# Row-64 key products, two weight cuts on GpSimd, and a looser order of cuts and PSUM banks in a four-layer fp32 block stack

## The reference

```
q = concat([q_nope, q_rope]); k = concat([k_nope, broadcast(k_rope)])     # 128 + 64 features
s = einsum('bhqd,bhkd->bhqk', q, k) / sqrt(192)
```

## Time and profile before

| what | us |
|---|---|
| median of three runs (3249.62 to 3250.29) | 3249.62 |
| the profiled execution | 3250.29 |
| its span | 3249.0 |
| PE busy | 3220.7 |
| DVE busy | 1823.7 |
| ACT busy | 1233.5 |
| POOL busy | 371.0 |

### The profile page before, as it was taken

One profiled execution on the slowest core, in us unless ns is written; L12 is line 12 of the kernel. 1 busy time (PEld: TensorE's weight loads), 2 busy tenths in 40 slices (PEclk: granted clock), 3 DMA queues, 4 the chain that ended last, 5 costly groups with the idle time before them and its releaser, 6 DMA issues.

```text
span 3249.0 us, 36841 instructions
## 1 busy us (share of the span) xinstructions
PE 3220.7 (99%) x15016; PEld 2673.2 (82%) x15016; DVE 1823.7 (56%) x2387; ACT 1233.5 (38%) x1838; POOL 371.0 (11%) x288
## 2 busy tenths in 40 slices
PE   8999999999999999999999999999999999999999
PEld 7788888888878888888888888888888888888887
DVE  3775556665477645666656643447545654345754
ACT  3222343344322333433444432226634442223642
POOL 1111211110011121111012000110012000011001
PEclk9999999999999999999999999999999999999999
DMA  4223332326422323232642232222332122222222
GB/s 159 68 78 104 98 110 78 104 98 209 155 72 72 109 86 117 78 104 91 205 147 66 79 98 89 94 91 93 101 135 66 64 95 93 93 98 91 91 94 99
DMA packets 93639, 330.84 MB, mean 102 GB/s; under 512 B 10560, under 2 KB 10816, under 8 KB 92704
## 3 DMA queue, kind: packets, MB, share of 16 engines
q1 hardware_dynamic: 90144, 313.90, 29.1%
q0 software_dynamic: 3328, 14.59, 1.3%
HBM read 326.35 MB, written 2.10 MB: 101 GB/s over the span
## 4 chain that ended last, share of the span: by engine, by line
PE 99%; DVE 1%; DMA 0%; ACT 0%; issue 0%; SPq 0%; POOL 0%; DVEq 0%
PE ps L458 98%; PE ps L809 1%; PE ps L564 1%; DMA raw<-wst 0%; DVE f L1486 0%; DVE wl L1367 0%; ACT wh L922 0%; DVE f L1435 0%; SPq L2107 0%; DVE h L1493 0%; DVE f L1474 0%; DVE X L1477 0%; ACT r L996 0%; ACT f L1162 0%; ACT f L1003 0%
## 5 line engine op out<-in xcount | busy, mean ns | idle before, releaser
L458 PE MATMUL ps<-h,wh 128*128 128x512 f32 (+1 forms) x5824 | 1709.4, 378 | 3.2 <-DVE wl L1367 1.1
L458 PEld LDWEIGHTS ps<-h,wh 128*128 128x128 f32 x5824 | 1068.8, 189 | 204.7 <-issue 10.5
L458 PE MATMUL ps<-h,wl 128*128 128x512 f32 (+1 forms) x2912 | 1095.4, 376 | 0.0
L1367 DVE TENSOR_TENSOR wl<-raw,wh 128x1024 fp32r<-128x1024 f32 (+3 forms) x596 | 751.0, 1272 | 353.1 <-ACT wh L922 352.1
L922 ACT CAST wh<-raw 128x1024 fp32r<-128x1024 f32 (+3 forms) x596 | 594.9, 1009 | 717.0 <-PE ps L458 708.0
L458 PEld LDWEIGHTS ps<-h,wl 128*128 128x128 f32 x2912 | 550.2, 189 | 99.6
L458 PE MATMUL ps<-r,wh 128*128 128x512 f32 x1632 | 505.5, 391 | 0.0
L458 PEld LDWEIGHTS ps<-r,wh 128*128 128x128 f32 x1632 | 305.4, 188 | 64.3 <-issue 1.9
L458 PE MATMUL ps<-r,wl 128*128 128x512 f32 x816 | 317.6, 389 | 0.0
L996 ACT CAST r<-f 128x512 fp32r<-128x512 f32 x182 | 112.1, 620 | 510.5 <-DVE f L1674 148.8
L458 PE MATMUL ps<-wh,r 128*128 128x512 f32 x960 | 304.6, 392 | 0.3
(11 more groups left out here) (147 smaller groups left out, 2101.3 us busy)
## 6 DMA issues: line engine op xcount, KB each, us to landing
raw<-wst SPq DMA_DIRECT2D x544, 512.0 KB, 3.3
raw<-wst SPq DMA_DIRECT2D x48, 320.0 KB, 2.8
f<-gains POOLq DMA_DIRECT2D x6, 1024.0 KB, 5.2
raw<-wst SPq DMA_DIRECT2D x16, 384.0 KB, 3.1
f<-tab POOLq DMA_DIRECT2D x16, 256.0 KB, 4.4
X<-x_in SPq DMA_DIRECT2D x4, 512.0 KB, 8.3
f<-gmb POOLq DMA_DIRECT2D x4, 512.0 KB, 4.7
raw<-wst SPq DMA_DIRECT2D x8, 256.0 KB, 2.7
```

The source lines that it names most:

```text
L458: return e.matmul(o, a, b, start=start, stop=stop, skip_group_check=True)
L1367: e.tensor_tensor(l[:, 0:WIDTH[c]], raw[:, c % NRAW, 0:WIDTH[c]], h[:, 0:WIDTH[c]].bitcast(F32), ALU.subtract).then_inc(*lo_cut.up(("lo", c)))
```

## The change

1. In `scores`, the product with k's low half takes only the 64 rows of this head, of both operands. (The product of q's low half with k's low half falls away with it.)
2. At the two exits of the feed-forward part the low halves of e1 and e3 are made on POOL, with a semaphore of their own, between the roots; DVE skips them, and one of its calls moves (the cut of e0+2 now comes ahead of row 3's mean).
3. The turn of the banks is no longer set after `early_second`. The held banks of gateb_1 and gateb_2 are let go together in front of the gate projection b and no longer inside its loop.
4. The calls that cut ahead are gone: upg3 and upv3 in the first two steps of the feed-forward part, and in the recurrence those of four chunks ahead in each step, on ACT and on DVE.
5. The steps of the layer norm of the 31-tap branch stand two chunks later.

```
@@ -283,7 +283,7 @@
         put(t, f"{L}/sc0", [[], [("centre", L, 3)], [("ret_squares", L)], [("ret_root", L)]]
             + [[("ret_out", L, h)] for h in range(4)])
         put(t, f"{L}/q0", [[("tap", L, k)] for k in range(30, -1, -1)])
-        put(t, f"{L}/gate0_7", [[("ln_sum", L)], [], [("ln_centre", L)], [], [], [("ln_root", L)], [("ln_spread", L)]]
+        put(t, f"{L}/gate1_0", [[("ln_sum", L)], [], [("ln_centre", L)], [], [], [("ln_root", L)], [("ln_spread", L)]]
             + [[("ln_out", L, j)] for j in range(4)])
     for L in (2, 3):
         put(t, f"{L}/ckv1", [[("n_squares", L, "q")], [("n_squares", L, "k")], [("n_root", L, "q")],
@@ -294,6 +294,9 @@
 
 BESIDE = beside()
 
+
+
+POOL_LOW = {NAME[EARLY[B][n]] for B in (2, 4) for n in (1, 3)}
 
 
 
@@ -415,12 +418,12 @@
         s_raw = [sem(f"s_raw{i}") for i in range(NRAW)]
         s_out = sem("s_out")
         group_done = Signal(sem("s_group_done"))
-        hi_cut, lo_cut = (Signal(sem(n)) for n in ("s_hi_cut", "s_lo_cut"))
+        hi_cut, lo_cut, lo_cut_pool = (Signal(sem(n)) for n in ("s_hi_cut", "s_lo_cut", "s_lo_cut_pool"))
         act_tile, act_hi, act_square = (Signal(sem(n)) for n in ("s_act_tile", "s_act_hi", "s_act_square"))
         dve_tile, dve_lo, dve_tap, dve_col = (Signal(sem(n)) for n in ("s_dve_tile", "s_dve_lo", "s_dve_tap",
                                                                        "s_dve_col"))
         pool_tile, pool_sum, pool_col = (Signal(sem(n)) for n in ("s_pool_tile", "s_pool_sum", "s_pool_col"))
-        signals = [group_done, hi_cut, lo_cut, act_tile, act_hi, act_square, dve_tile, dve_lo, dve_tap,
+        signals = [group_done, hi_cut, lo_cut, lo_cut_pool, act_tile, act_hi, act_square, dve_tile, dve_lo, dve_tap,
                    dve_col, pool_tile, pool_sum, pool_col]
         loads = {}
 
@@ -550,7 +553,6 @@
                         if a:
                             banks.let_go(name)
                             last.then_inc(*group_done.up(("done", name), ("closed", NAME[name])))
-                banks.turn = banks.of["tr", B, 2, 0]
 
             def turn_rows(B, t):
 
@@ -641,8 +643,6 @@
                 if first == 0:
                     tile(f"{L}/gate{g}_0", xs)
                 for j in range(8):
-                    if 1 < j <= first:
-                        banks.let_go(f"{L}/gate{g}_{j - 1}")
                     if j < 7 and j + 1 >= first:
                         tile(f"{L}/gate{g}_{j + 1}", xs)
                     key = ("pr", L, b, j)
@@ -785,6 +785,7 @@
                         tile(f"{L}/gateb_{h - 5}", xs, hold=h > 5)
 
                 def scores(h):
+                    part = slice(64 * (h % 2), 64 * (h % 2) + 64)
                     qr, (kr_h, kr_l) = R(QR_AT[h // 2][h % 2]), (R(i) for i in KR_AT)
                     w.wait_ge(*at("qn", L, h))
                     w.wait_ge(*at("kn", L, h))
@@ -796,7 +797,7 @@
                         o = take(("s", L, h, i))
                         three(o[:, 0:n], R(55)[:, b], R(56)[:, b], R(57)[:, 0:n], R(58)[:, 0:n], True, False)
                         mm(o[:, 0:n], qr[:, b], kr_h[:, 0:n], False, False)
-                        mm(o[:, 0:n], qr[:, b], kr_l[:, 0:n], False, True).then_inc(
+                        mm(o[:, 0:n], qr[part, b], kr_l[part, 0:n], False, True).then_inc(
                             *group_done.up(("done", ("s", L, h, i))))
 
                 def turn(h):
@@ -860,6 +861,8 @@
                                 last.then_inc(*group_done.up(("done", ("va", L, n, t)), *closes))
                             elif closes:
                                 last.then_inc(*group_done.up(*closes))
+                banks.let_go(f"{L}/gateb_1")
+                banks.let_go(f"{L}/gateb_2")
                 gate_proj(L, "b", "b", "b", pair(16, 24, 8), ("b_lo", L), first=3)
                 for nm in ("u", "za"):
                     tile(f"{L}/{nm}0", xs)
@@ -1130,8 +1133,6 @@
                         e.activation(F(60 + 3 * (j % 3) + m), bank(key), ACT.Copy,
                                      scale=vec1(L, "fcw", 3 * (22 * m + j) + 2)[:, 0:1]).then_inc(
                             *act_tile.up(("f_tap", L, j, m, 0)))
-                    if j < 2:
-                        cut(NAME[f"{L}/upg3"] + j)
                     if j == NF - 1:
                         cut(NAME[f"{L}/dn0_3"])
                     w.wait_ge(*at("f_tap", L, j, 0, 2))
@@ -1300,10 +1301,8 @@
                         w.wait_ge(*at("a", L, j))
                         e.activation(r, r, ACT.Exp, scale=cc[:, 10 + j:11 + j], bias=cc[:, 10 + j:11 + j]).then_inc(
                             *act_tile.up(("a2", L, j)))
-                        cut(NAME[f"{L}/lru{j}"] + NSP)
                         w.wait_ge(*at("done", f"{L}/zc{j}"))
                         e.activation(z, bank(f"{L}/zc{j}"), ACT.Tanh, scale=0.5).then_inc(*act_tile.up(("zc_tanh", L, j)))
-                        cut(NAME[f"{L}/zc{j}"] + NSP)
 
                     def root(t):
                         j = 5 * hf + t
@@ -1362,10 +1361,11 @@
                 while cut_at[0] <= min(upto, len(CHUNKS) - 1):
                     c = cut_at[0]
                     cut_at[0] += 1
-                    w.wait_ge(*at("hi", c))
-                    h, l = split_at(c)
-                    e.tensor_tensor(l[:, 0:WIDTH[c]], raw[:, c % NRAW, 0:WIDTH[c]], h[:, 0:WIDTH[c]].bitcast(F32),
-                                    ALU.subtract).then_inc(*lo_cut.up(("lo", c)))
+                    if c not in POOL_LOW:
+                        w.wait_ge(*at("hi", c))
+                        h, l = split_at(c)
+                        e.tensor_tensor(l[:, 0:WIDTH[c]], raw[:, c % NRAW, 0:WIDTH[c]], h[:, 0:WIDTH[c]].bitcast(F32),
+                                        ALU.subtract).then_inc(*lo_cut.up(("lo", c)))
 
             def slot(name):
                 cut(NAME[name] + LA)
@@ -1516,15 +1516,13 @@
                     mean(B, 2, "y")
                     cut(e0)
                     renew(B, 2)
-                    cut(e0 + 1)
+                    cut(e0 + 2)
                     mean(B, 3, "y")
                     mean(B, 2, "x")
-                    cut(e0 + 2)
                     renew(B, 3)
                     h_out(B, 2)
                     mean(B, 3, "x")
                     h_out(B, 3)
-                    cut(e0 + 3)
                     h_lo(B, 2)
                     h_lo(B, 3)
                     cut(e0 + 5)
@@ -1982,6 +1976,13 @@
                     e.tensor_tensor(mv[:, 3:4], mv[:, 2:3], half[:, 0:1], ALU.pow).then_inc(
                         *pool_col.up(("root", "va", L, i)))
 
+            def cut_low(c):
+
+                w.wait_ge(*at("hi", c))
+                h, l = split_at(c)
+                e.tensor_tensor(l[:, 0:WIDTH[c]], raw[:, c % NRAW, 0:WIDTH[c]], h[:, 0:WIDTH[c]].bitcast(F32),
+                                ALU.subtract).then_inc(*lo_cut_pool.up(("lo", c)))
+
             def roots(B, *which):
                 for kind, t in which:
                     m = 2 if kind == "y" else 6
@@ -2011,7 +2012,9 @@
                     return
                 roots(B, ("x", 0), ("x", 1), ("y", 2))
                 if B in FFN:
+                    cut_low(NAME[EARLY[B][1]])
                     roots(B, ("y", 3), ("x", 2))
+                    cut_low(NAME[EARLY[B][3]])
                 else:
                     roots(B, ("x", 2), ("y", 3))
                 roots(B, ("x", 3))
```

16 lines of the change are left out of this document (4 added, 12 removed).

## The result

The kernel after takes 3307.69 us in the median (3305.17 to 3309.79, four runs), the kernel before 3249.62 (3249.15 to 3250.29, four runs): slower by 58.1 us, ratio 1.0178, 95% interval 1.0161 to 1.0196. Forecast were 3296 and a range up to 3306, so direction and most of the mechanisms are right and 12 us are missing. The profiled execution of the kernel after has 3310.41 us, 60.1 more than that of before and 2.7 more than its own median.

The account below looks back on a forecast made before the run. PE, busy 99% of the span, was taken as the bound, so added PE work or waits count whole. Terms 22.3 + 9.4 + 1.7 + 5.0 + 4.4 + 3.6 = +46.4 gave 3296 us, range 3280 to 3306.

Parts of the forecast that it names:

- The 64-row product: In 16 attention heads, each step between 128 and 64 rows costs PE 0.20 us; 1.39 a head, +22.3 us.
- rival 1: In the heads' scores, 64 rows are free in fp32r: sum 24.1, 3274 us; chance 0.1.
- The wait at projection b: Layers 2 and 3: PE waits for ACT to read gateb_1's bank, 4.7 us with a load; twice, +9.4.
- The entries: Two feed-forward entries: PE waits 1.2 at upg2 and 1.9 at upg3, less 0.6 before upg4; +5.0 us.
- rival 3: At the feed-forward exits POOL and DVE run side by side: sum 40.9, 3290 us; chance 0.12.
- The exits: Two feed-forward exits: POOL's cuts and DVE's sums exclude each other, PE's transposes wait 2.2 us each; +4.4.
- After the early stages: First tile after boundaries 2, 4 and 5 waits for an early tile's bank, 0.4, 0.65 and 0.65; +1.7 us.
- The recurrence: Two halves in two layers: the chunk after the fifth zc is cut 0.9 us late; 4 x 0.9 = +3.6.
- Rival 2: ACT and DVE keep up, so neither late cuts nor banks are seen: sum 26.7, 3276 us; chance 0.12.
- rival 4: Whole kernel not slower: moved banks quicken PE's 512-column products, 3244 us at 4 ns each; chance 0.03.
- At nothing: the layer norm's steps two chunks later: 31-tap branch's norm: PE waits for none of these steps, whose last result is due three tiles later; 0 us.
- Rival 5: Across the kernel, more stalls than found, each like one of those forecast: 3310 us; chance 0.08.

Follow-up runs that it names:

- e1: Kernel before with only the 64-row key-low product of `scores` taken from the change: 3272.92 us, +23.1 (ratio 1.0071).
- e2: As e1, but every second row block starts with its 64-row product, giving half the steps between row counts: 3262.00 us, +12.2 (ratio 1.0037).
- e5: Kernel before with only the low cuts on POOL at the two feed-forward exits, their semaphore and the moved DVE call: 3255.27 us, +5.0 (ratio 1.0015).
- e6: As e5, but each POOL cut is two instructions of 512 columns: 3250.22 us, 0.0 against the kernel before (ratio 1.0000).
- e3: Kernel before with only gateb_1 and gateb_2 let go together ahead of projection b: 3264.29 us, +14.5 (ratio 1.0045).
- e7: Kernel before with only the calls that cut ahead removed (feed-forward entries and recurrence): 3263.66 us, +13.4 (ratio 1.0039).
- e8: Kernel before without the reset of the banks' turn and with the layer norm's steps two chunks later: 3253.74 us, +3.5 (ratio 1.0012).
- e4: As e3, but PE fills most of each wait with 20 products of 512 columns that nobody reads: 3259.48 us, +9.7 (ratio 1.0029).
- e11: Kernel before with the retention norm's 32 one-column products spread among the next tile's products: 3250.14 us, +0.4 (ratio 0.9999).
- e9: As e6, but DVE's moved call stays where the kernel before has it: 3251.08 us, +1.2 against the kernel before (ratio 1.0003).
- e10: As e9, but the feed-forward entry cuts ahead in three steps in place of two: 3248.43 us, -1.5 against the kernel before (ratio 0.9995).

## Why the prediction was right and where it was wrong

**Right in mechanism and size.** The 64-row product: 22.3 forecast, 23.1 alone (e1); e2 shows that it is the step. So rival 1, that 64 rows are free in fp32r, falls: a 64-row product between 128-row ones costs 0.36 us more and none is faster. The 2x that the Trainium skill (TensorEngine Tiling (Array Packing), Theoretical Speedup) allows for a dimension of 64 or less does not come to such a product; the page speaks of tiles that work beside each other, and no run here tries that. The wait at projection b: 4.7 forecast, 4.8 and 0.3 for loads. The entries: 1.2 and 1.9 forecast, 1.3 and 2.0 measured. POOL's cuts: 2.4 forecast, 2.42 measured; rival 3, both engines side by side, falls with e5 and e6. The exits: 2.2 forecast each, 1.8 and 1.7 without the slow products. After the early stages 1.7 against 2.0. The recurrence 0.9 against 1.1 each. Rival 2 (late cuts and banks are not seen, 3276) falls with e3, e7 and e8, and rival 4 too: PE's pace between the waits is that of before (three products in 0.68).

**Wrong: each stall was priced at its own length.** The step is "Stall 4.6, with 0.1 for an uncovered load 4.7, twice: +9.4", and the same in the terms for the entries and exits. Behind such a wait PE works at half its clock for some microseconds, and that is added whole. It is 4.8 us at projection b (e3 less e4: 14.5 - 9.7; the same in the trace of the kernel after), and in that trace 3.5 at the exits and 1.7 at an entry: 10.0 of the 13.7 us by which the trace's 60.1 exceed the 46.4. At projection b e4 shows the cause; at the exits and the entry the trace shows the slow products behind the waits, and no run fills those waits. The 1.2 of layer 1's retention comes on top and is scatter. The trace of before could have warned. Its windows show the clock at 0.50 behind the one-column products, but the 40 slices of the PEclk row round that away, and the prediction rests on those.

Windows of the kernel before, first retention:

```profile
182.50:186.00 3.50, 3.50 (x10) 2.74 (x9) 3.17 (x6) 0.00 (x0) 2.84 (x1) 0.51 0.42 150
```

**Wrong: "At nothing: the layer norm's steps two chunks later".** I asked when its result is needed, not whose bank it holds. The norm's spread result sits in a PSUM bank until DVE's fourth ln_out step has read it (L1421, 362.67 to 363.41); two chunks later the walk comes back to that bank first, and the product at 362.79 waits until 363.55. Twice 0.9 with the load; e8's trace has it at the same place.

**Rival 5** (more stalls than found, 3310) came nearest in time, but not in kind: the stalls were found, but for the norm's two. That its price was near is luck.

The four runs of the kernel after scatter over 4.6 us, the four of before beside them over 1.1 and the 26 beside e5 to e8 over 2.0. That they differ in how many half-clock stretches they catch fits (e11's two clusters lie 1.8 apart, about the 1.5 to 1.9 that such a stretch costs there), but is argued, not shown: only one run of each kernel has a trace.

## What to carry to other kernels

Where PE is the bound, price a stall as its length plus the slow products behind it, and read the granted clock in windows of a few microseconds behind each stall that is there already. Put products with equal row counts next to each other, and where POOL and DVE both read two operands from SBUF at the same time, split POOL's instruction into pieces. Before moving a step, ask which bank its result holds and when the walk comes back to it; and where two edits feed one late chain, run each alone as well as both, since their costs do not add.

## What the runs showed of the hardware

- After a wait of 5.0 us (from PE's last start to its next) the granted clock was 0.50 at every one of four places (two in the kernel after, two in e3), after 3.6 us at both places (e7), after 2.2 us at one entry and not at the other (kernel after), and with 20 products in the wait at neither (e4). At the exits it was 0.50 after waits of 2.1 and, eight transposes later, 1.2 us at all four places (kernel after, e5), and 1.00 where only the 1.2 was left, at all six (e6, e9, e10).
- The half-clock stretches do not need an idle PE: 32 products of one column in 3.6 us are followed by one as well (182.5 in the kernel before).
- A sum on DVE with both inputs in SBUF took 0.69 us alone and 2.46 to 2.66 beside a POOL subtraction of 2.42 (kernel after, e5); beside halves of 1.31 it took 1.02 to 1.55 (e6, e9, e10).
- fp32r with 64 rows costs on each step to or from 128 rows about what fp32 does in the earlier trace rows (0.20): e1's 64 products, two steps each, cost 23.1 us, 0.18 for a step.
